# The four sums of each block's up weights made by GpSimd instead of VectorE, in a decoder step on one core

## The reference

```python
x = layer_norm(ALPHA * x + h @ w_out, ln1_g, ln1_b)
u = jax.nn.relu(x @ w_up)                                   # w_up   (2048, 8192)
return layer_norm(ALPHA * x + (u * u) @ w_down, ln2_g, ln2_b)   # w_down (8192, 2048)
```

## Time and profile before

| | us |
|---|---|
| median of 3 executions | 3115.44 |
| profiled execution, device time | 3104.12 |
| its span, first to last instruction | 3102.4 |
| TensorE busy / weight loads busy | 2852.7 / 2680.2 |
| VectorE busy | 1864.3 |
| ScalarE busy | 837.8 |
| GpSimd busy | 200.9 |
| the 120 sums of weights (L1903) on VectorE | 146.4 |

### The profile page before, as it was taken

One profiled execution on the slowest core, in us unless ns is written; L12 is line 12 of the kernel. 1 busy time (PEld: TensorE's weight loads), 2 busy tenths in 40 slices (PEclk: granted clock), 3 DMA queues, 4 the chain that ended last, 5 costly groups with the idle time before them and its releaser, 6 DMA issues. The chain is left out here.

```text
span 3102.4 us, 58889 instructions
## 1 busy us (share of the span) xinstructions
PE 2852.7 (92%) x25791; PEld 2680.2 (86%) x25791; DVE 1864.3 (60%) x2177; ACT 837.8 (27%) x1225; POOL 200.9 (6%) x200
## 2 busy tenths in 40 slices
PE   5999999999997597799789999999999999999995
PEld 5998888889876366599689999999999999999994
DVE  2265555455541486523667777777777777777775
ACT  2221222122211254311533322322322223223221
POOL 0011110111100320011000000000000000000002
PEclk8999999999998699799889999999999999999997
DMA  8489999999987722144213233233233233233232
GB/s 327 133 300 377 390 400 407 408 400 406 400 334 249 212 90 89 30 138 126 76 55 109 74 90 109 70 95 109 69 96 103 72 99 103 72 100 103 71 100 85
DMA packets 339185, 548.61 MB, mean 177 GB/s; under 512 B 20043, under 2 KB 243884, under 8 KB 329122
## 3 DMA queue, kind: packets, MB, share of 16 engines
q1 hardware_dynamic: 318194, 388.33, 37.8%
q0 software_dynamic: 13104, 141.33, 11.2%
q10 hardware_dynamic: 7632, 15.20, 1.3%
HBM read 508.96 MB, written 35.84 MB: 176 GB/s over the span
## 5 line engine op out<-in xcount | busy, mean ns | idle before, releaser
L330 PE MATMUL prj_G<-prj_xh,prj_wh 128*128 128x280 f32 x1696 | 507.9, 299 | 27.0 <-DVE prj_wl L544 27.0
L1900 DVE SCALAR_TENSOR_TENSOR hT<-big_G,hT 128x544 f32<-128x544 f32 x512 | 367.3, 722 | 228.0 <-PE big_G L1736 226.7
L332 PE MATMUL prj_G<-prj_xh,prj_wl 128*128 128x280 f32 x1696 | 501.7, 296 | 0.0
L331 PE MATMUL prj_G<-prj_xl,prj_wh 128*128 128x280 f32 x1696 | 501.4, 296 | 0.0
L551 DVE STREAM_TRANSPOSE prj_kT<-prj_k_nat 128x4096 f32<-128x4096 f32 x64 | 284.5, 4445 | 336.7 <-PE prj_S L363 336.7
L1813 ACT ACTIVATE wh<-raw 128x1024 fp32r<-128x1024 f32 x228 | 240.2, 1058 | 676.9 <-PE big_G L1736 562.3
L1734 PE MATMUL big_G<-ff_uh,wh 128*128 128x272 f32 x1360 | 396.5, 292 | 19.5 <-DVE hT L1900 10.0
L1735 PE MATMUL big_G<-ff_ul,wh 128*128 128x272 f32 x1360 | 393.8, 290 | 0.0
L1736 PE MATMUL big_G<-ff_uh,wl 128*128 128x272 f32 x1360 | 393.3, 289 | 0.0
L330 PEld LDWEIGHTS prj_G<-prj_xh,prj_wh 128*128 128x128 f32 x1696 | 326.6, 193 | 54.6 <-issue 30.8
L1887 DVE TENSOR_TENSOR wl<-raw,wh 128x1024 fp32r<-128x1024 f32 x228 | 278.6, 1222 | 119.5 <-ACT wh L1813 119.4
(11 more groups left out here) (393 smaller groups left out, 5996.9 us busy)
## 6 DMA issues: line engine op xcount, KB each, us to landing
prj_v_nat<-in_cache_v SPq DMA_DIRECT2D x256, 512.0 KB, 6.9
raw<-in_w_down SPq DMA_DIRECT2D x128, 512.0 KB, 4.4
raw<-in_w_up SPq DMA_DIRECT2D x120, 512.0 KB, 5.2
prj_raw<-in_w_in SPq DMA_DIRECT2D x106, 512.0 KB, 12.7
raw<-in_w_out SPq DMA_DIRECT2D x16, 1024.0 KB, 6.2
prj_scratch<-prj_stage ACTq DMA_DIRECT2D x53, 280.0 KB, 7.2
out_xr<-x_scratch SPq DMA_DIRECT2D x16, 544.0 KB, 7.2
mix_att<-prj_scratch SPq DMA_DIRECT2D x24, 280.0 KB, 3.4
```

Of the source, the lines that this page charges most:

```text
L330: mm(out, w_hi[:, k, m], xh[:, k0 + k, cols], start=(first and k == 0), stop=False)
L331: mm(out, w_hi[:, k, m], xl[:, k0 + k, cols], start=False, stop=False)
L332: last = mm(out, w_lo[:, k, m], xh[:, k0 + k, cols], start=False, stop=(end and k == nk - 1))
L1900: V.scalar_tensor_tensor(out, G[2 + t % 2][:, :, 0:HALF_M], 1.0 / ALPHA, out, ALU.mult, ALU.add).then_inc(y_done, 1)
```

## The change

A semaphore `weight_sum` is added. The four sums of each of the 30 blocks leave VectorE's program, with the waits that stood ahead of them, and GpSimd gets a program that makes them in the same order, each waiting for the one before. ScalarE's `high` waits on the new semaphore.

```diff
+        @block.gpsimd
+        def _(po):
+
+            def combine(out, in0, in1, op):
+                nc.gpsimd.tensor_tensor(out, in0, in1, op).then_inc(weight_sum, 1)
+
+            for b in range(1, NBLK - 1):
+                base, sums = FIRST + NCH * (b - 1), 4 * (b - 1)
+                for q in (0, 2):
+                    po.wait_ge(raw_full[q], 32 * b)
+                combine(Q[2], Q[0], Q[2], ALU.subtract)
+                po.wait_ge(weight_sum, sums + 1)
+                po.wait_ge(lo_done, base + 3)
+                combine(Q[3], Q[3], Q[2], ALU.subtract)
+                po.wait_ge(weight_sum, sums + 2)
+                combine(Q[0], Q[0], Q[3], ALU.add)
+                po.wait_ge(weight_sum, sums + 3)
+                combine(Q[1], Q[1], Q[3], ALU.subtract)
...
-                    ac.wait_ge(sum_done, sums)
+                    ac.wait_ge(weight_sum, sums)
...
                 u_low(b)
-                dv.wait_ge(raw_full[2], 32 * b)
-                combine(Q[2], Q[0], Q[2], ALU.subtract)
-                dv.wait_ge(sum_done, sums + 1)
-                dv.wait_ge(lo_done, base + 3)
-                combine(Q[3], Q[3], Q[2], ALU.subtract)
                 low(base + 3, phase + 3, 3)
-                dv.wait_ge(sum_done, sums + 2)
-                combine(Q[0], Q[0], Q[3], ALU.add)
                 low(base + 4, phase + 4, 0)
...
                 low(base + 5, phase + 5, 2)
-                combine(Q[1], Q[1], Q[3], ALU.subtract)
                 low(base + 6, phase + 6, 1)
```

More of the change, by code:

```diff
@@ L1678, in phase_ff @@
         raw_full = [sem(f"raw_full{i}") for i in range(4)]
-        (hi_done, lo_done, up_done, sum_done, copied, added, relu_done, uh_done, low_done, down_ps, y_done, turned) = (
-            sem(x) for x in ("hi_done lo_done up_done sum_done copied added relu_done uh_done low_done down_ps y_done turned".split()))
+        (hi_done, lo_done, up_done, sum_done, copied, added, relu_done, uh_done, low_done, down_ps, y_done, turned, weight_sum) = (
+            sem(x) for x in ("hi_done lo_done up_done sum_done copied added relu_done uh_done low_done down_ps y_done turned weight_sum".split()))
         block = ctx.enter_context(nc.Block())
@@ L1854, in ff_block @@
             def ff_block(b, phase):
-                sums, ups, downs = NSUM + 4 * (b - 1), DOWN + UP * (b - 1), KT * (b - 1)
+                sums, ups, downs = 4 * (b - 1), DOWN + UP * (b - 1), KT * (b - 1)
                 high(phase, 0, 2 * b, downs=downs + 8)
@@ L1965, in ff_block @@
             def ff_block(b, base, phase):
-                sums, ups = NSUM + 4 * (b - 1), DOWN + UP * (b - 1)
+                ups = DOWN + UP * (b - 1)
                 add(b - 1, 8)
```

## The result

Six executions of the changed kernel have a median of 3132.86 us (3123.72 to 3137.20), six of the kernel before 3111.40 (3105.00 to 3120.93). The ratio is 1.0063, 95% interval 1.0039 to 1.0088: slower by 0.63%, about 20 us. The forecast was 36 us. The sign was right, and so was one of the two places on which the cost was put; the other, 16 us of the 36, cost nothing.

The account below looks back on a forecast made before the run. TensorE was taken to bound the loop; 19.5 us at products 3 and 4 plus 16.3 at relu_square made +36 us, so the median of 3115.4 would become 3151 us, the forecast's own range 3128 to 3170.

Parts of the forecast that it names:

- What bounds the loop: Feed-forward loop: TensorE bounds it, busy 1379.47 of 1400.47 us; relieving VectorE brings at most 6 us.
- 2.36 us a sum: GpSimd's time for one 128x1024 sum, 0.22 us of it fixed; four take 9.4 us a block.
- Mutual lock: GpSimd sums and VectorE instructions with two SBUF inputs block each other, whichever starts second waiting; the forecast's case, chance 0.55.
- The one-sided rival: VectorE waits for GpSimd but never the reverse; product 4 gains 6 us, relu_square costs 16: 3125 us, chance 0.12.
- Products 3 and 4: Start of block: low 3 and low 4 held behind GpSimd sums delay TensorE 0.65 us a block, 19.5 us.
- Sum 1 against relu_square: Late in the block: sum 1 starts first in 45% of 29 blocks, holding relu_square and delaying tile 4; 16.3 us.
- the 0.35 at tile 6: TensorE's loss at down tile 6, waiting for add 4 after low 10; disappears where relu_square is held.
- The sum: Whole execution: 19.5 us at the block's start plus 16.3 at relu_square, 36 us slower.

Follow-up runs that it names:

- e6_early: Kernel before, all sums on VectorE, next block's sum 1 moved between adds 5 and 6: ratio 0.9975, loop -8.8 us.
- e1_sum3: Kernel before with sum 3 alone on GpSimd: ratio 1.0053, loop +15.6 us.
- e3_hold: Kernel before plus one 1024-column GpSimd instruction a block, timed just ahead of relu_square: ratio 1.0070, loop +25.8 us.
- e4_sum1: Kernel before with sum 1 alone on GpSimd, the other three on VectorE: ratio 1.0002.
- e7_early10: e6_early with low 10 moved behind add 4 and sum 1 between adds 6 and 7: ratio 0.9892, loop -19.1 us.
- e2_order: Changed kernel, four sums on GpSimd, u_low after low 3, sum 4 after low 4, high 4 ahead of bank 0's copy: ratio 1.0056 to kernel before.
- e5_order5: e2_order with sum 4 only after low 5 instead of low 4: ratio 1.0028 to kernel before.

## Why the prediction was wrong in size

- **What bounds the loop: right.** Of ScalarE's 60 waits for the sums before, product 6 never waited behind the 30 ahead of high 6; the 30 ahead of high 4 stand in the chain of product 4 and cost its 0.19 us a block. The most that VectorE's relief could bring was put at 6 us; e6_early has that part at product 4, 5.7 us, and another 3.2 at tile 2 (below).
- **2.36 us a sum: right**, 2.40 alone (e1_sum3, sum 3 above).
- **Mutual lock: right.** Sum 2's 3.31 us behind u_low and sum 4's 3.26 behind low 3 are the rows that were missing. The one-sided rival falls. For a held sum only 0.14 of its start is hidden (2.40 less the 2.26 after u_low's end), where I had left it open from 0 to 0.22.
- **Products 3 and 4: 19.5 us forecast, 24.3 measured**, 0.81 a block instead of 0.65, inside the ends of 13.5 and 29. The ends of sums 2, 3 and 4 and of lows 3 and 4 were given as 3.42 to 3.64, 5.88 to 6.10, 9.10 to 9.54, 6.96 to 7.18 and 10.18 to 10.62; they came at 3.54, 6.02, 9.35, 7.10 and 10.44.
- **Sum 1 against relu_square: the step that failed.** 16.3 us were put on it (45% of 29 blocks at 1.25) and it cost nothing: in no block was sum 1 ahead. Its price is confirmed by e3_hold, and by e4_sum1's 7 blocks (11.0 / 7 less the 0.35 at tile 6 is 1.22, forecast 1.25); what was wrong is when Q[2] lands, and with it how often sum 1 is ahead. The closest block:

```profile
2514.36 1.28 DVE L1909 SCALAR_TENSOR_TENSOR small<-small 128x1088 f32<-128x1088 f32 x1
```

```profile
2514.52 3.38 POOL L1733 TENSOR_TENSOR raw<-raw 128x1024 f32<-128x1024 f32 x1 [14.58 <-DMA raw<-in_w_up]
```

 There GpSimd was 0.16 us late. The reasoning was that low 6 would come earlier and leave less queued ahead of Q[2], and that Q[2] would land in 4.3. Low 6 did come earlier (13.06 us of the block against 14.67), but it releases two down loads, which then were on their way together with the one that low 5 had released. That one landed late, high 8 waited for it, and low 8, which releases the load of Q[2], waited for high 8. In the block whose u_low starts at 2064.28, high 8 and the load of Q[2]:

```profile
2081.53 1.06 ACT L1832 ACTIVATE wh<-raw 128x1024 fp32r<-128x1024 f32 x1 [1.88 <-DMA raw<-in_w_down]
```

```profile
L1700 SPq DMA_DIRECT2D raw<-in_w_up x1: 368/368/368, 2083.9 to 2083.9; - x1
...
DMA to landing us min/median/max: 5.0/5.0/5.0
```

 Counted from product 4 as the prediction counts, Q[2] was issued at 18.8 instead of 18.45 and landed at 23.8, not 22.75. The late issue is 0.35 us of that; the greater part, 0.7, is that the load took 5.0 us and not 4.3. The same over all 29 blocks: issued at 18.7 and landed at 23.6 (medians), the earliest at 23.0, where relu_square begins at 22.98. Counted from u_low, which is 0.81 more, sum 1 began at 23.94 to 25.41, relu_square at 23.77 to 24.21.

 The 4.3 had been misread in the rows of the kernel before. The u_low of that load's block is this row:

```profile
2000.47 1.28 DVE L1894 TENSOR_TENSOR ff_ul<-small,ff_uh 128x1088 fp32r<-128x1088 f32 x1
```

 The load, at 2019.9, was thus issued at 19.4 of its block and landed at 23.7, no earlier than the other one of the earlier trace rows; a landing of 4.3 counted from an issue at 18.45 joins two blocks. In none of the 29 blocks of the kernel before did Q[2] land ahead of 23.66 (median 23.9). And the earlier low 6 brought little: the last down load was issued 2.4 us earlier (12.7 against 15.1, medians) but landed only 0.45 earlier (19.9 against 20.4), and Q[2] 0.3 earlier, where some 0.9 was needed. I followed what the earlier low 6 did to the issues, but not to the landings of the loads in flight. e4_sum1, where low 6 stays 3.5 us behind low 5 as in the kernel before (1.1 in the changed one), has Q[2] issued at 18.35 and landed in 4.5 us (median), early enough in 7 blocks: there the reckoning would have held, at 24% of the blocks.
- **Not forecast: -2.9 us at tile 2.** At tile 2 the kernel before lost 1.04, 1.93 and 2.36 us in three blocks with a late down load, instead of 0.69, 3.3 us more in all; the changed one had one such block, 0.4 more. In e3_hold, with the kernel before's order on VectorE, tile 2 stands at 24.7 too, and at 20.9 to 21.3 in e1_sum3, e4_sum1, e6_early and e7_early10; whether the order does that or chance isn't shown.
- **The base.** The median of the kernel before went from 3115.4 of three executions to 3111.4 of six, so the forecast of 3151 stood 4 us too high on top of that.
- **The sum.** 36 forecast, 4.8 too little at products 3 and 4, 16.3 too much at relu_square, 2.9 gained at tile 2: 21.4. That the measured 3132.86 lies in the forecast's own range of 3128 to 3170 is in part luck, since the 4.8 us too little made up for some of the 16.3 too much.

The rule named in the prediction (the Trainium skill, "SBUF — State Buffer", "Who interferes with whom"), an exclusive lock between a VectorE instruction with two SBUF inputs and a GpSimd one that reads SBUF, holds here in both directions: the trace agrees, with 1.08 to 1.14 us after GpSimd's end for VectorE and 2.25 to 2.26 us after VectorE's end for GpSimd.

## What to carry to other kernels

Work taken from an engine that isn't the bound brings only what the bound engine waits for; add up its gaps by place first, for here 40 us lay in three of them and were won by reordering VectorE, with no work moved. On GpSimd an elementwise sum of two SBUF tiles took twice as long (2.40 us against 1.22), and a VectorE instruction with two SBUF inputs that started meanwhile ended only its own length behind it: look for what stands beside it, and at how much the engine behind has to spare. Where a cost depends on which of two events comes first, and they are tenths of a microsecond apart, follow the whole chain that sets both, loads in flight among them, and take a load's issue and its landing from the same block.

## What the runs showed that I had not expected

Loads of 512 KB that are issued closer together take longer to land, with the same bytes. The third and fourth down load of a block took 4.1 and 5.3 us from issue to landing in the kernel before, 6.2 and 7.2 in the changed one, where low 6 follows low 5 by 1.1 us instead of 3.5, 6.0 and 7.1 in e2_order, and 4.1 and 5.3 again in e5_order5 (medians). ScalarE's waits for them are the poorer sign: 27.4, 59.7 and 107.8 us, but also 65.9 in e5_order5, where TensorE lost little by them at tile 2. And VectorE at 1015.71 us of 1360.25, 75% busy, is enough to keep TensorE without a gap when its order is right.
